# State products around the spreading, k products behind the read-out, and GpSimd's order, in an RWKV-7 state stage

## The reference

```python
def step(state, inp):
    rt, wt, kt, vt, kkt, at = inp
    sa = jnp.einsum('bhvk,bhk->bhv', state, -kkt)
    state = (state * wt[:, :, None, :]
             + sa[..., :, None] * (kkt * at)[..., None, :]
             + vt[..., :, None] * kt[..., None, :])
    yt = jnp.einsum('bhvk,bhk->bhv', state, rt)
    return state, yt
_, y = lax.scan(step, s0, xs)
# then per head: mean and variance of y, y = (y - mean) * rsqrt(var + GN_EPS), y * gn_g + gn_b, + bonus * v
```

## Time and profile before

| | us |
|---|---|
| median of 3 runs | 4813.63 (4811.77 to 4820.19) |
| profiled execution | 4808.79 |
| its span, first to last instruction | 4807.0 |
| TensorE busy in the span | 4312.6 (90%) |
| VectorE, ScalarE, GpSimd busy | 2576.5 (54%), 1319.3 (27%), 599.1 (12%) |
| mean granted TensorE clock | 0.953 |

### The profile page before, as it was taken

The page is one execution under the profiler, slowest core; times in us unless marked ns, Lnnn a source line. Parts: engine busy times, 40 slices in busy tenths (PEclk is TensorE's granted clock), DMA queues, the critical chain, the costliest instruction groups (busy, mean ns, idle before and its releaser), DMA issues. The chain is left out here.

```text
span 4807.0 us, 68650 instructions
## 1 busy us (share of the span) xinstructions
PE 4312.6 (90%) x25232; PEld 3586.1 (75%) x25232; DVE 2576.5 (54%) x5011; ACT 1319.3 (27%) x2626; POOL 599.1 (12%) x585
## 2 busy tenths in 40 slices
PE   8999789998699968999979996999979799799879
PEld 6777677887577748888877885778768677677667
DVE  4344434444466656777764334787733433567733
ACT  3232222222222211111111113666621211322211
POOL 0000012211000002333330110000000111012100
PEclk9999899999899979999989998999989999999989
DMA  3111321111533330101132225210034323422233
GB/s 126 59 61 50 123 70 59 63 66 49 178 127 128 128 129 30 47 31 46 46 107 87 110 109 165 82 36 19 10 132 156 122 104 122 130 86 93 91 121 113
DMA packets 218307, 434.14 MB, mean 90 GB/s; under 512 B 36419, under 2 KB 90436, under 8 KB 218022
## 3 DMA queue, kind: packets, MB, share of 16 engines
q1 hardware_dynamic: 218150, 432.08, 26.4%
HBM read 248.40 MB, written 146.93 MB: 82 GB/s over the span
## 5 line engine op out<-in xcount | busy, mean ns | idle before, releaser
L236 PE MATMUL rp_pj<-rp_w_high,rp_hT_high 128*128 128x512 f32 (+1 forms) x640 | 238.7, 382 | 27.7 <-DVE rp_w_low L228 15.0
L236 PE MATMUL fp_pj<-fp_w_high,fp_hT_high 128*128 128x512 f32 (+2 forms) x640 | 220.1, 358 | 31.1 <-DMA fp_ident<-const_ident 21.8
L2518 DVE TENSOR_SCALAR_CACHE_REDUCE fa_sm<-fa_sc 128x512 f32<-128x512 f32 (+2 forms) x320 | 194.4, 610 | 91.2 <-PE fa_sc L2359 80.2
L237 PE MATMUL rp_pj<-rp_w_low,rp_hT_high 128*128 128x512 f32 (+1 forms) x640 | 233.1, 373 | 0.0
L236 PE MATMUL hg_pj<-hg_w_high,hg_hT_high 128*128 128x512 f32 x512 | 211.1, 412 | 16.7 <-DVE hg_w_low L228 16.7
L237 PE MATMUL fp_pj<-fp_ahead_w_low,fp_hT_high 128*128 128x512 f32 (+2 forms) x640 | 217.4, 354 | 0.0
L236 PE MATMUL rc_pj<-rc_w_high,rc_hT_high 128*128 128x512 f32 (+1 forms) x512 | 191.6, 382 | 23.3 <-DMA rc_ident<-const_ident 12.7
L237 PE MATMUL hg_pj<-hg_w_low,hg_hT_high 128*128 128x512 f32 x512 | 206.2, 403 | 0.0
L2373 PE MATMUL fa_tp<-fa_ident,fa_sm 128*128 128x128 f32 x1088 | 175.7, 282 | 31.5 <-DVE fa_pT_low L178 14.9
L2466 ACT CAST fa_pT_high<-fa_tp 128x512 fp32r<-128x512 f32 (+1 forms) x288 | 161.1, 560 | 147.9 <-PE fa_tp L2373 145.7
L178 DVE TENSOR_TENSOR fa_pT_low<-fa_tp,fa_pT_high 128x512 fp32r<-128x512 f32 (+1 forms) x288 | 188.9, 656 | 14.7 <-ACT fa_pT_high L2466 14.4
(11 more groups left out here) (560 smaller groups left out, 11259.2 us busy)
## 6 DMA issues: line engine op xcount, KB each, us to landing
rw_given<-rw_packed_dram SPq DMA_DIRECT2D x48, 512.0 KB, 4.0
rc_back<-rc_XB SPq DMA_DIRECT2D x48, 336.0 KB
rw_packed_dram<-rp_M SPq DMA_DIRECT2D x48, 256.0 KB, 2.6
rp_M<-rp_U SPq DMA_DIRECT2D x16, 728.0 KB, 4.7
hg_xt<-in_x SPq DMA_DIRECT2D x16, 512.0 KB, 3.8
kept_x_high_dram<-hg_hT_high SPq DMA_DIRECT2D x16, 512.0 KB, 3.5
kept_x_low_dram<-hg_hT_low SPq DMA_DIRECT2D x16, 512.0 KB, 4.3
sw_hT_high<-kept_x_high_dram SPq DMA_DIRECT2D x16, 512.0 KB, 3.6
```

What stands on the lines that cost most here:

```text
L236: pe.matmul(out, hT.high[:, kc, :], high[:, kc, lo:hi], start=kc == 0, stop=False)
L237: pe.matmul(out, hT.high[:, kc, :], low[:, kc, lo:hi], start=False, stop=False)
L2518: dve.tensor_scalar(sm[:, to:to + cols], bank_of(slot)[:, 0:cols], 0.0, NEG, ALU.add, ALU.max, accum_out=tops[:, four, c:c + 1]).then_inc( ...
```

## The change

Three orders are changed, with the banks and waits that they need. On TensorE, Z is issued right behind the b products and Y between the two halves of the spreading, so `solve` takes one of them per call; the k products of the new tile, both halves, go behind the read-out, into banks 6 and 7 (when the rows spread there have been read, a new semaphore `half_read`) and 4 and 5 (when SA and y are copied out of them). The k·v matmuls go behind the SA matmuls. Of the fillers four of the first eight stay, and none of the twelve. On VectorE, the decay of S opens the step, and the four masks of KA come behind the inversion and `renew_state`, ahead of `put_out`. On GpSimd, gain and the first operation of rest come ahead of the corners, and the last two of rest wait for `XT_first`. The turning of the next kk waits for the eight masks instead of the copies of SA and y.

```diff
-        PRODUCT_BANKS = (((0, 1), (2, 3)), ((4, 5), (0, 1)))
+        PRODUCT_BANKS = (((0, 1), (2, 3)), ((6, 7), (4, 5)))
...
-                if two == 0 and t is not None:
-                    pe.wait_ge(SA_ready, t + 1)
-                    pe.wait_ge(y_ready, t + 1)
+                if two == 0 and i is not None:
+                    pe.wait_ge(masked, 8 * i + 8)
...
-                if i is not None:
-                    pe.wait_ge(masked, 8 * i + 8)
-                for p in range(PAIRS):
-                    ... B[INC_BANK][:, cols], given_of(pt, "k")[:, cols], V[:, cols] ...
                 pe.wait_ge(XT_ready, PER_TILE * (t + 1))
...
                 last.then_inc(SA_done, 1)
+                if i is not None:
+                    pe.wait_ge(masked, 8 * i + 2)
+                for p in range(PAIRS):
+                    ... B[INC_BANK][:, cols], given_of(pt, "k")[:, cols], V[:, cols] ...
...
                     multiply(i, pi, 0, 1)
-                    multiply(i, pi, 1, 0)
-                    for n in range(8 if m else 0):
+                if m:
+                    solve(t, pt, 0)
+                if pr:
+                    for n in range(4 if m else 0):
                         ... filler ...
                     spread(i, 0)
-                    pe.wait_ge(masked, 8 * i + 2)
-                    multiply(i, pi, 1, 1)
+                if m:
+                    solve(t, pt, 1)
+                if pr:
                     pe.wait_ge(masked, 8 * i + 4)
                     spread(i, 1)
                 if m:
-                    if pr:
-                        pe.wait_ge(masked, 8 * i + 6)
-                    solve(t, pt)
                     read_out(t, pt, i)
                 if pr:
-                    if not m:
-                        pe.wait_ge(masked, 8)
-                    for n in range(12 if m else 0):
-                        ... filler ...
+                    pe.wait_ge(half_read, i + 1)
+                    multiply(i, pi, 1, 0)
+                    if m:
+                        pe.wait_ge(SA_ready, t + 1)
+                        pe.wait_ge(y_ready, t + 1)
+                    multiply(i, pi, 1, 1)
                     for g in range(2):
                         turn_first(i, pi, g)
...
     (GpSimd)
-                if pr:
-                    ... corner(FIRST, 0), corner(FIRST, 1) ...
                 if m:
                     ... gain; rest = v x bonus ...
+                if pr:
+                    ... corner(FIRST, 0), corner(FIRST, 1) ...
+                if m:
                     pool.drain()
+                    if pr:
+                        pool.wait_ge(XT_first, i + 1)
                     ... rest + gn_b; rest x gate ...
...
     (VectorE)
+                if m:
+                    dve.wait_ge(vg_here[pt], 48 * (ht + 1))
+                    decay(pt, 0).then_inc(S_in, 1)
                 if pr:
                     compact_blocks(i)
                     for r in range(2):
                         mask_products(i, pi, 0, r)
-                    mask_products(i, pi, 1, 0)
-                if m:
-                    dve.wait_ge(vg_here[pt], 48 * (ht + 1))
-                    decay(pt, 0).then_inc(S_in, 1)
-                if pr:
-                    mask_products(i, pi, 1, 1)
                     dve.drain()
...
                     renew_state(t, pt)
+                if pr:
+                    for r in range(2):
+                        mask_products(i, pi, 1, r)
```

More of the change, by code:

```diff
@@ L1439, in rwkv @@
             "products", "masked", "first_turned", "X_ready", "XT_ready"))
-        parts_ready, spread_done, XT_first = (sem(n) for n in ("parts_ready", "spread_done", "XT_first"))
+        parts_ready, spread_done, half_read, XT_first = (sem(n) for n in ("parts_ready", "spread_done", "half_read", "XT_first"))
         CT_ready, T1_done, T1_ready, corr_done = (sem(n) for n in ("CT_ready", "T1_done", "T1_ready", "corr_done"))
@@ L1597, in read_out @@
                 last.then_inc(SA_done, 1)
+                if i is not None:
+                    pe.wait_ge(masked, 8 * i + 2)
+                for p in range(PAIRS):
+                    cols = slice(p * P, (p + 1) * P)
+                    pe.matmul(B[INC_BANK][:, cols], given_of(pt, "k")[:, cols], V[:, cols], start=p == 0, stop=False)
                 pe.wait_ge(SA_ready, t + 1)
@@ L1701, in corner @@
                     pool.tensor_tensor(CT[:, 4 * g:4 * g + 4, :], BA[pi][:, 4 * g:4 * g + 4, 0, :], again(blocks[:, l - FIRST, :], 4), ALU.mult).then_inc(CT_ready, 1)
-                if pr:
-                    for g in range(2):
-                        pool.wait_ge(masked, 8 * i + 2 * g + 2)
-                        corner(FIRST, g)
                 if m:
@@ L1712, in step @@
                     pool.tensor_tensor(heads(rest[pt][:], RW_HEADS), heads(given_of(pt, "v"), RW_HEADS), spread(bonus[pt][:], RW_DIM), ALU.mult)
+                if pr:
+                    for g in range(2):
+                        pool.wait_ge(masked, 8 * i + 2 * g + 2)
+                        corner(FIRST, g)
+                if m:
                     pool.drain()
+                    if pr:
+                        pool.wait_ge(XT_first, i + 1)
                     pool.tensor_tensor(rest[pt][:], rest[pt][:], gn_b[:], ALU.add)
```

36 lines of the change are left out of this document (17 added, 19 removed).

## The result

The changed kernel takes 4737.9 us (4726.5 to 4742.0), the kernel before 4812.7 in the same comparison (4805.9 to 4820.2). The ratio is 0.984, with an interval from 0.9817 to 0.9863: 75 us less, 8.6 under the predicted 4746.5 and inside the range. The profiled execution has a span of 4740.2, 66.8 shorter than before; it is the longest of the four that were timed.

The account below looks back on a forecast made before the run. VectorE's work before the inversion and the last twelve fillers, in series, were taken to set the tile's first half. Gains of 57.4 (tiles 2 to 15), 5.4, 3.6 and 0.7, together 67.1, from 4813.6 gave 4746.5 us; range 4718 to 4790.

Parts of the forecast that it names:

- VectorE ahead of the inversion: VectorE's step head: decay hidden, KA masks moved behind, so the inversion starts at T=8.09 instead of 11.22, 3.13 us earlier.
- The inversion: VectorE's small-block inversion: 9.97 us instead of 10.74, being tile 0's 9.27 plus 0.7 for meeting the second corner.
- TensorE up to the turning: TensorE's first half: without the 12 fillers or the SA wait, turning starts at T=19.4, before 24.76; gain 5.36 per tile.
- What is late next: VectorE behind the inversion: masks and slowed sums on S make TensorE's second level wait 1.3; net gain 4.06 per tile.
- the two readings between which the prediction chose: VectorE-GpSimd meetings: by the exclusion rule the sums on S pay some 1.4; by the 0.83 row alone, 0.3.
- The clock: TensorE's granted clock: as many tiles as before with one 1.2 GHz stretch; none at all would gain 15 us more.
- Tile 0 and the last step: Stage's ends: tile 0 gains 3.6, masks and a wait gone but corner met; last step gains 0.7, SA wait gone.
- The likeliest case: Whole program: the forecast of 4746.5, 4735 to 4760 by itself, chance 0.50.
- the first (VectorE isn't late): Second half of the tile: GpSimd costs S little or slack absorbs it, 18 us more gained, 4728; chance 0.17.
- The second (the second half eats more): Second level: one further 1.2 GHz stretch per tile, or VectorE's chain a microsecond longer; gain 42, 4772; chance 0.23.
- The slower one: TensorE's clock doesn't come back without fillers: at 0.76 in every tile, 134 us at the low clock, 4881; chance 0.06.
- no new wait holds TensorE to the old pace: TensorE, rival of no effect: a wait placed too early keeps the old pace, time within 0.2%; chance 0.04.

Follow-up runs that it names:

- e7: Changed kernel, with GpSimd's gain waiting until the decay of S is done: 4731.6 us, ratio 0.984.
- e11: Kernel before, with only GpSimd's new order: 4813.1 us, ratio 1.000.
- e9: e5, with the last two operations of rest waiting for the renewed state instead of XT_first: 4717.9 us, ratio 0.980.
- e1: Changed kernel with GpSimd's old order, corners first and no wait for XT_first: 4764.5 us, ratio 0.990.
- e4: Changed kernel with the k·v matmuls ahead of the SA product again, so that y waits for SA: 4733.7 us, ratio 0.984.
- e3: Kernel before, with only the twelve fillers behind the read-out left out: 4779.2 us, ratio 0.993.
- e2: Changed kernel with the twelve fillers put back, between the new tile's k products and the turning of XT: 4757.2 us, ratio 0.988.
- e10: Changed kernel with four fillers between Z and Y in the last step alone: 4730.1 us, ratio 0.983.
- e5: Changed kernel with put_out moved from VectorE to the head of GpSimd's step, gain and first of rest to the end of its step before: 4718.7 us, ratio 0.981.
- e8: Changed kernel without its last four fillers: 4755.3 us, ratio 0.989.
- e12: Kernel before, with GpSimd's new order and without the twelve fillers: 4793.3 us, ratio 0.996.

## Why the prediction was right

**VectorE ahead of the inversion.** Masks and decay did leave the path: the inversion starts at T=8.05 in one half of the tiles, 8.09 predicted. In the other half it starts at 8.50. There the decay was not hidden: the prediction put it at nothing and did not ask what it meets in its new place, which is gain, put by the change itself at the head of GpSimd's step. 0.44 in seven tiles, 3 us (e7).

**The inversion.** 9.91 against 9.97 by my sum. One step waits for the corner (1.08 against 0.98), and the others are free. Two small errors meet in this: the 9.27 of tile 0 is not the least (e11, with nothing beside the inversion, takes 8.96; tile 0 has an idle stretch of 0.39 inside), and the corner costs 0.80 where I took 0.7.

**TensorE up to the turning.** Predicted T=19.4, found 19.27 and 19.69. The profile marks no idling between 0 and the turning, and y starts without a wait.

**What is late next.** The two sums on S lost 1.27 against 1.4, the first X was ready at T=28.25 against 28.3, the second level started at T=28.41 against 28.35. Its delay from the turning on was 1.05, or 1.01 in the other tiles, against 1.3, and the turning came at 19.27 or 19.69 in place of 19.4. e9, e1 and e7 turn the meetings on and off by placing GpSimd's operations. The Trainium skill's rule in SBUF — State Buffer, section Who interferes with whom, agrees with these rows: the sums paid as in the long rows of the prediction. But the short row, the decay of 0.83 at 2102.95, was read wrongly. It was not cheap for having been issued first: the second corner beside it ends at 2103.23, and the decay 0.55 behind that, as the three operations after do. It found only 0.28 of the corner left. So the two readings between which the prediction chose are one, and what decides is how much of GpSimd's operation is left.

**The sum at full clock.** Tiles 1 to 14: 14 x 42.2=590.8 before, 531.8 after, 59.0 less; predicted 5.4+13 x 4.1=58.7. Tiles 2 to 14 take 38.05 on average, predicted 38.1.

**The clock.** This term was mis-sized: "I take it that as many tiles as before have one stretch at 1.2 GHz". There was none, and 15.0 us more came in (605.8 before less 590.8). The prediction had this as a bound, not as its case. The new wait in front of the second level didn't bring the clock down. That the other cause which I named, the wait for SA in the read-out, had done it before is only partly so: put back (e4) it gives three such stretches, in three tiles, not in eight. What else in the old order did is open; that the twelve fillers behind the read-out did not prevent it, and that it became rarer without them (e3), is shown.

**Tile 0 and the last step.** Predicted 3.6 and 0.7 of gain, with 4.1 for tile 15. Tile 0 gave 0.4: its products started at the low clock (24.0 us of the tile against 20.5). The last period took 58.4 instead of 54.8, a loss of 3.6 where I had 4.8 of gain, since the last step ran at 0.57 of the clock; before, 12.6 us from 2482 on were at 1.00. In the profiles of e2, e4, e7 and e10, which have the same order in these two places or nearly so, tile 0 takes 38.1 to 39.9 and the last period 49.9 to 56.6, so the changed kernel's profile is at the unlucky end of both.

In all, the stage (first product to last matmul) is 70.8 shorter in the profile: 59.0 from the order, 15.0 from the clock in the tiles, 0.4 in tile 0, less 3.6 at the end. The rest of the program gave 4 back, in stages that the change doesn't touch. That the span is 66.8 shorter, against 67.1 predicted, is luck: the 15.0 that the prediction left out are paid for by 3.2 less in tile 0, 8.4 less at the end and these 4. The order's part, 59.0 against 58.7, is no luck of this kind, though within the tile 1.05 and 1.01 stand for 1.3 and the delayed decay for nothing.

The likeliest case was right in mechanism and size at full clock. Of the rivals, the first (VectorE isn't late) is excluded by the waits at 2158.25 and 2163.29 and by e5, which gained just by relieving VectorE. The second (the second half eats more) did not come: there is no low stretch in tiles 1 to 14, and X was ready when predicted. The slower one is real, but it takes the last four fillers out (e8), which the change left in. And no new wait holds TensorE to the old pace.

What the parts are worth, per tile at full clock: fillers 1.45 alone (e3); GpSimd's order nothing alone (e11) and nothing with the fillers out (e12), but 1.15 in the new order (e1); the rest of 42.2 to 38.05, some 1.5, comes with the products and masks in their new places. How these 1.5 divide between TensorE's order and VectorE's no run shows, since none has one without the other, and none takes out the other four fillers by themselves.

## What to carry to other kernels

When several engines' orders are changed at once, a part may be worth nothing alone, as GpSimd's was here (e11, e12): find which queue ends last after each, with the operations queued ahead of the one that is waited for, before pricing the next. Place GpSimd's operations beside what VectorE reads from PSUM, and not only away from the old victim: ask which operations with two operands in SBUF they will meet in the new place, and how much of GpSimd's will be left then. In this kernel fillers paid where TensorE would idle among narrow matmuls and nothing waited behind them (e8), and only cost where the turning stood in series with them (e2, e3). And when a sum comes out right, check it term by term: here four misses cancelled.

## What the runs showed of the hardware

A fall of the clock can last long with TensorE at work. In e8 a stretch of idling of about a microsecond behind 2.7 us of narrow matmuls was followed by 20.5 us at 1.2 GHz while TensorE worked mostly on 64- and 128-column matmuls; in the kernel before the clock came back after 3.4 us in seven cases of eight. Why it stayed low is not shown. Twelve 512-column fillers behind the old read-out went with 30.7 us at 1.2 GHz in the tiles, their absence with 13.7 (e3); four between Z and the spreading of the new order went with none, their absence with 88.7 (e8), in one execution of each.

A 128x512 operation of VectorE with two operands in SBUF that finds GpSimd inside a 128x512 operation of its own ends 0.55 behind it, whatever was left: the decay of 0.83 before, 1.42, 1.05 and 1.60 after, 1.75 and 1.60 in e12 (2226.23 and 2227.91, where GpSimd's operations end at 2225.68 and 2227.36). Beside the end of rstd, 128x8, the decay at 2173.17 after took 0.69, no more than alone. So it costs nearly nothing near the end of GpSimd's operation and about a microsecond near its start. It gets in between two operations of GpSimd that follow each other, and GpSimd pays then too: in the tile after, the second operation of rest took 1.53 where it takes 1.28 in e9. And a small one is held too: in the tile after, the scaling of the mean, 128x8, took 0.81 beside a corner (0.17 in the kernel e9, where no corner had started).
